# Two mixer entries of a fused transformer kernel: sums of squares by halves, a diagonal of roots, and vector lengths by products with ones

## What is computed

```python
x = x + hybrid_mixer(rmsnorm(x, norm_g[layer, 1]), ...)
def rmsnorm(x, g):
    y = xf * lax.rsqrt(jnp.mean(xf * xf, axis=-1, keepdims=True) + EPS)
    return y.astype(x.dtype) * g
```

```python
f = swiglu_ffn(rmsnorm_2(x, ffn1_norm_pre[i]), ffn1_w_in[i], ffn1_w_out[i])
x = x + 0.5 * rmsnorm_2(f, ffn1_norm_post[i])
h = rmsnorm_2(x, mix_norm_pre[i])
p = h @ mix_w_in[i]
...
def l2norm(x):
    return x * lax.rsqrt(jnp.sum(x * x, axis=-1, keepdims=True) + 1e-6)
q = l2norm(q.reshape(b, l, GDN_HEADS, GDN_DK)) * (GDN_DK ** -0.5)
k = l2norm(k.reshape(b, l, GDN_HEADS, GDN_DK))
```

## Time and profile before

| | |
|---|---|
| median of 3 runs | 2804.7 us (2804.18 to 2805.13) |
| the profiled execution | 2807.67 us |
| its span in the trace | 2805.9 us |
| TensorE busy | 2735.0 us, 97% |
| ScalarE / VectorE / GpSimd busy | 1459.5 / 1588.1 / 899.6 us |
| mean granted clock of TensorE | 0.99 |
| HBM read | 446.06 MB, 159 GB/s over the span |

### The profile page before, as it was taken

How to read it: one execution, slowest core, us unless ns; L and a number is a source line. 1 busy time by engine, 2 the same in 40 slices (tenths; PEclk the granted TensorE clock), 3 DMA queues, 4 the chain that set the end, 5 groups by cost and what they waited for, 6 DMA issues and landing times.

```text
span 2805.9 us, 46606 instructions
## 1 busy us (share of the span) xinstructions
PE 2735.0 (97%) x17368; PEld 2363.6 (84%) x17368; DVE 1588.1 (57%) x2439; ACT 1459.5 (52%) x2134; POOL 899.6 (32%) x469
## 2 busy tenths in 40 slices
PE   9999999999999999999989999999999899999999
PEld 7879897888878997878879898878788798998787
DVE  5543854545535845545546586555455465856554
ACT  5545655445444655445445644655454456446543
POOL 0017663000027665010037554710100375547200
PEclk9999999999999999999999999999999999999999
DMA  6655445655555446656557542466565575424664
GB/s 215 186 176 147 136 150 173 187 180 181 187 161 155 133 148 194 187 173 192 187 136 195 114 91 77 147 193 186 180 188 187 136 195 113 91 71 144 193 187 143
DMA packets 368442, 450.01 MB, mean 160 GB/s; under 512 B 32526, under 2 KB 266128, under 8 KB 368240
## 3 DMA queue, kind: packets, MB, share of 16 engines
q1 hardware_dynamic: 366768, 445.82, 54.4%
q10 hardware_dynamic: 544, 0.95, 0.1%
q0 software_dynamic: 928, 0.45, 0.1%
HBM read 446.06 MB, written 1.05 MB: 159 GB/s over the span
## 4 chain that ended last, share of the span: by engine, by line
PE 90%; DVE 4%; ACT 3%; POOL 2%; issue 1%; DMA 0%; SPq 0%; DVEq 0%; ACTq 0%
PE PS L515 27%; PE PS L517 26%; PE PS L516 26%; POOL wl L551 2%; PE PS L671 1%; DVE PS L2119 1%; ACT wh L543 1%; PE PS L1082 1%; PE PS L648 1%; PE PS L1149 1%; ACT xh L1290 1%; PE PS L780 1%; PE PS L1017 1%; PE PS L1008 1%; PE PS L1139 1%
## 5 line engine op out<-in xcount | busy, mean ns | idle before, releaser
L551 POOL TENSOR_TENSOR wl<-ring,wh 128x1024 fp32r<-128x1024 f32 (+1 forms) x348 | 835.6, 2419 | 1706.5 <-ACT wh L543 1705.2
L543 ACT ACTIVATE wh<-ring 128x1024 fp32r<-128x1024 f32 x848 | 890.8, 1056 | 906.5 <-PE PS L515 863.7
L551 DVE TENSOR_TENSOR wl<-ring,wh 128x1024 fp32r<-128x1024 f32 x500 | 611.4, 1225 | 620.4 <-ACT wh L543 620.1
L515 PE MATMUL PS<-wh,xh 128*128 128x512 f32 x1600 | 633.0, 396 | 22.3 <-DVE xl L1807 14.0
L517 PE MATMUL PS<-wh,xl 128*128 128x512 f32 x1600 | 622.5, 389 | 0.0
L516 PE MATMUL PS<-wl,xh 128*128 128x512 f32 x1600 | 621.6, 389 | 0.0
L515 PE MATMUL PS<-xh,wh 128*128 128x256 f32 x1888 | 554.9, 294 | 1.8 <-DVE xl L1807 1.7
L516 PE MATMUL PS<-xl,wh 128*128 128x256 f32 x1888 | 539.6, 286 | 0.0
L517 PE MATMUL PS<-xh,wl 128*128 128x256 f32 x1888 | 539.5, 286 | 0.0
L515 PEld LDWEIGHTS PS<-xh,wh 128*128 128x128 f32 x1888 | 367.4, 195 | 22.8 <-issue 16.1
L515 PEld LDWEIGHTS PS<-wh,xh 128*128 128x128 f32 x1600 | 301.0, 188 | 88.6 <-issue 20.6
(11 more groups left out here) (294 smaller groups left out, 2615.4 us busy)
## 6 DMA issues: line engine op xcount, KB each, us to landing
ring<-in_ffn_w_in_dram SPq DMA_DIRECT2D x352, 256.0 KB, 3.0
ring<-in_mix_w_in_dram SPq DMA_DIRECT2D x256, 256.0 KB, 3.8
ring<-in_w_in_dram SPq DMA_DIRECT2D x200, 256.0 KB, 3.0
ring<-in_ffn_w_gate_dram SPq DMA_DIRECT2D x176, 256.0 KB, 2.9
ring<-in_ffn_w_up_dram SPq DMA_DIRECT2D x176, 256.0 KB, 3.1
ring<-in_ffn_w_down_dram SPq DMA_DIRECT2D x176, 256.0 KB, 2.7
ring<-in_ffn_w_out_dram SPq DMA_DIRECT2D x176, 256.0 KB, 2.8
ring<-in_w_branch_dram SPq DMA_DIRECT2D x32, 256.0 KB, 2.8
```

The lines of the kernel that those rows point to most:

```text
L515: first_ = mm(o, w[0], x[0], start=start, stop=False, skip_group_check=True)
L543: act_(dst, src, ACT.Copy).then_inc(hi_ready, 1)
L551: (engine or v_).tensor_tensor(dst, src, part_views(t, wh)[0], ALU.subtract).then_inc(lo[t.slot()], 1)
```

## The change

- The sum of squares of a tile is taken in two halves of 512 columns, in the mixers' entries and in `act_post`. The first half's sum gets the constant eps by an Identity and is then the bias of the Ln over the second half's sum. In `dve_post` each half's product with `post` waits for its own half's square.
- `dve_scale` goes. ScalarE multiplies the identity by the roots (a diagonal, 128x128, in `sq`), and TensorE computes each block as a product of `x` with this diagonal in place of a transposition of the scaled tile.
- In the second mixer's entry one of the two `high` moves behind the second tile's `stats`.
- The lengths: a product of a 128x128 matrix of ones with two heads' squares gives the sums on all partitions at once, in bank 4, twice per group (after the first and after the second tile). ScalarE takes Ln and Exp over 128x512 in place, and `unit` reads the bank. `pick` and `spread` go. The table load stands ahead of the wait for the sums. VectorE's `short` is cut in two, with the first `unit` between.

```diff
+        def diag(q):
+            return sqt[:, q, 0:P]
...
-        def pe_xt_mix(pe, s, m):
-            for q in range(QT):
-                pe_xt(pe, s, q, sqt, lambda h: pe.wait_ge(xn_made, 4 * m + 2 * q + 1 + h))
+        def pe_xt_mix(pe, s, tr, q):
+            pe.wait_ge(tr[1].sem, tr[1].at(f"mix.{q}.diag"))
+            for k in range(KB):
+                ins = mm(xt_bank(q, k), x[:, q, k * P:(k + 1) * P], diag(q), start=True, stop=True)
+                if k % 4 == 3:
+                    ins.then_inc(xt_done, 1)
...
-            def sums(n):
+            def sums(j):
+                n = j // 2
                 pe.wait_ge(m2[1].sem, m2[1].at(f"l2sq{n}"))
...
-                for h in range(4):
-                    ins = mm(PS[0:4, 4, 0:S], pick[:, 3 - h:7 - h], sq[:, 4 * (n % 2) + h, :], start=(h == 0), stop=(h == 3))
-                ins.then_inc(m2[0].sem, m2[0].did(f"l2s{n}"))
-            def spread(j):
...
                     pe.wait_ge(m2[2].sem, m2[2].at(f"l2n{j - 1}"))
...
+                mm(bank(4), ones, sqp(2 * (n % 2) + j % 2), start=True, stop=True).then_inc(
+                    m2[0].sem, m2[0].did(f"l2s{j}"))
...
-                group(f"QKV{n}", (n + 1) % 2 * 2, {0: lambda: sums(n - 2), 2: lambda: spread(2 * n - 4), 3: lambda: spread(2 * n - 3)})
+                group(f"QKV{n}", (n + 1) % 2 * 2, {0: lambda: sums(2 * n - 4), 1: lambda: sums(2 * n - 3)})
...
-            act_sum(e, tr, f"{tag}.ss{q}", 2 + q, PS[:, 2 * q:2 * q + 2, :].rearrange("p b n -> p (b n)"),
-                    act2.rearrange("p a q c -> p (a q c)"), scale * D ** -0.5)
-            act_root(e, tr, lay, f"{tag}.ss{q}", f"{tag}.{q}", 2 + q, 1, consts[:, 2:3])
+                col = 2 + q if h else 6 + q
+                act_sum(e, tr, f"{tag}.ss{q}.{h}", col, bank(2 * q + h), means[:, h * HALF:(h + 1) * HALF], scale * D ** -0.5)
+                if h == 0:
+                    e.wait_ge(tr[1].sem, tr[1].at(f"{tag}.ss{q}.0", lay))
+                    act_(ss[:, col:col + 1], ss[:, col:col + 1], ACT.Identity, bias=consts[:, 0:1]).then_inc(
+                        tr[1].sem, tr[1].did(f"{tag}.se{q}"))
...
             def stats(q):
-                e.wait_ge(x_upd, 4 * s + 2 * q + 2)
-                act_sum(e, tr, f"mix.ss{q}", q, x[:, q, :], sqt[:, q, :], D ** -0.5)
-                act_root(e, tr, lay, f"mix.ss{q}", f"mix.{q}", q)
+                halves = ((4 + q, slice(0, HALF)), (q, slice(HALF, D)))
+                for h, (col, at) in enumerate(halves):
+                    e.wait_ge(x_upd, 4 * s + 2 * q + 1 + h)
+                    act_sum(e, tr, f"mix.ss{q}.{h}", col, x[:, q, at], sqt[:, q, at], D ** -0.5)
...
+                act_(r_, ss[:, q:q + 1], ACT.Ln, bias=ss[:, 4 + q:5 + q]).then_inc(tr[1].sem, tr[1].did(f"mix.{q}.ln"))
...
+                act_(r_, r_, ACT.Exp, scale=-0.5).then_inc(tr[1].sem, tr[1].did(f"mix.{q}.rstd"))
+                e.wait_ge(tr[1].sem, tr[1].at(f"mix.{q}.rstd"))
+                act_(diag(q), ident[:], ACT.Copy, scale=r_).then_inc(tr[1].sem, tr[1].did(f"mix.{q}.diag"))
             if post:
                 post(0)
-                high(e, t, 2)
+                high(e, t, 1)
                 stats(0)
                 post(1)
                 act_xh(e, s, 0, range(4), gain)
                 stats(1)
+                high(e, t, 1)
                 act_xh(e, s, 0, range(4, KB), gain)
...
-            def root(n):
-                e.wait_ge(m2[0].sem, m2[0].at(f"l2s{n}"))
...
-                tables(LN_EXP)
-                r_ = rstd[0:4, 0, 0:S]
-                act_(r_, PS[0:4, 4, 0:S], ACT.Ln, bias=consts[0:4, 0:1]).then_inc(m2[1].sem, m2[1].did(f"l2.{n}.ln"))
...
+            def root(j):
+                e.wait_ge(m2[0].sem, m2[0].at(f"l2s{j}"))
+                act_(bank(4), bank(4), ACT.Ln, bias=consts[:, 0:1]).then_inc(m2[1].sem, m2[1].did(f"l2.{j}.ln"))
...
             for n in range(6):
                 high(e, t, 1)
                 if n >= 2:
-                    root(n - 2)
-                high(e, t, 2)
+                    tables(LN_EXP)
+                    root(2 * n - 4)
+                high(e, t, 1)
+                if n >= 2:
+                    root(2 * n - 3)
+                high(e, t, 1)
+                if n >= 2:
+                    tables(SILU_TANH)
...
-        def dve_scale(e, tr, q):
...
-                short(n)
+                short(n, (0,))
                 if 1 <= n <= 4:
                     unit(2 * n - 2)
+                short(n, (2,))
+                if 1 <= n <= 4:
                     taps(2)
                     unit(2 * n - 1)
                     taps(3)
```

More of the change, by code:

```diff
@@ L199, in program @@
         post = sb("post", [D])
-        ss = sb("ss", [4])
+        ss = sb("ss", [8])
         rs = sb("rs", [4])
@@ L224, in program @@
         ones64, rot = masks[:, 6 * P:7 * P], masks[:, 7 * P:8 * P]
-        pick = sb("pick", [7])
         W = sb("W", [WIDE])
@@ L798, in pe_mix1 @@
                                 if (q, m) == (0, 1):
-                                    pe_xt(pe, s, 1, sqt, lambda h: pe.wait_ge(xn_made, 4 * lay + 2 + 1 + h))
+                                    pe_xt_mix(pe, s, first["norm"], 1)
                         t.k += 4
@@ L1247, in _ @@
                 pe_ffn(pe, t, first["ffn"], s, "f0", 1)
-                pe_xt(pe, s + 1, 0, sqt, lambda h: pe.wait_ge(xn_made, 4 * env.lay + 1 + h))
+                pe_xt_mix(pe, s + 1, first["norm"], 0)
                 pe_mix1(pe, t, first["mix"], first["soft"], s + 1, lay)
@@ L1258, in _ @@
                 pe_ffn(pe, t, second["ffn"], s, "f0", 2)
-                pe_xt_mix(pe, s + 1, LAYERS + lay)
+                for q in range(QT):
+                    pe_xt_mix(pe, s + 1, second["norm"], q)
                 pe_mix2(pe, t, s + 1)
@@ L1317, in act_mix_in @@
+            r_ = rs[:, 2 + q:3 + q]
+            e.wait_ge(tr[1].sem, tr[1].at(f"{tag}.ss{q}.1", lay))
+            act_(r_, ss[:, 2 + q:3 + q], ACT.Ln, bias=ss[:, 6 + q:7 + q]).then_inc(tr[1].sem, tr[1].did(f"{tag}.{q}.ln"))
+            e.wait_ge(tr[1].sem, tr[1].at(f"{tag}.{q}.ln", lay))
+            act_(r_, r_, ACT.Exp, scale=-0.5, bias=consts[:, 2:3]).then_inc(tr[1].sem, tr[1].did(f"{tag}.{q}.rstd"))
         def act_mix_in(e, t, tr, s, gain, post=None):
-            lay = env.lay
             def stats(q):
-                e.wait_ge(x_upd, 4 * s + 2 * q + 2)
-                act_sum(e, tr, f"mix.ss{q}", q, x[:, q, :], sqt[:, q, :], D ** -0.5)
-                act_root(e, tr, lay, f"mix.ss{q}", f"mix.{q}", q)
+                halves = ((4 + q, slice(0, HALF)), (q, slice(HALF, D)))
+                for h, (col, at) in enumerate(halves):
+                    e.wait_ge(x_upd, 4 * s + 2 * q + 1 + h)
+                    act_sum(e, tr, f"mix.ss{q}.{h}", col, x[:, q, at], sqt[:, q, at], D ** -0.5)
+                    if h == 0:
+                        e.wait_ge(tr[1].sem, tr[1].at(f"mix.ss{q}.0"))
+                        act_(ss[:, col:col + 1], ss[:, col:col + 1], ACT.Identity, bias=consts[:, 0:1]).then_inc(
+                            tr[1].sem, tr[1].did(f"mix.se{q}"))
+                r_ = rs[:, q:q + 1]
+                e.wait_ge(tr[1].sem, tr[1].at(f"mix.ss{q}.1"))
+                act_(r_, ss[:, q:q + 1], ACT.Ln, bias=ss[:, 4 + q:5 + q]).then_inc(tr[1].sem, tr[1].did(f"mix.{q}.ln"))
+                e.wait_ge(tr[1].sem, tr[1].at(f"mix.{q}.ln"))
+                act_(r_, r_, ACT.Exp, scale=-0.5).then_inc(tr[1].sem, tr[1].did(f"mix.{q}.rstd"))
+                e.wait_ge(tr[1].sem, tr[1].at(f"mix.{q}.rstd"))
+                act_(diag(q), ident[:], ACT.Copy, scale=r_).then_inc(tr[1].sem, tr[1].did(f"mix.{q}.diag"))
@@ L1518, in square @@
                 if n >= 2:
[L1519 removed]
+                    e.wait_ge(m2[0].sem, m2[0].at(f"l2s{2 * n - 3}"))
                 e.wait_ge(m2[1].sem, m2[1].at(f"silu{n}"))
@@ L1794, in step @@
             e.wait_ge(tr[2].sem, tr[2].at(name))
-        def dve_scale(e, tr, q):
-            e.wait_ge(tr[1].sem, tr[1].at(f"mix.{q}.rstd"))
-            for b in (2 * q, 2 * q + 1):
-                v_.tensor_scalar(tok(sqt, b), tok(x, b), rs[:, q:q + 1], None, ALU.mult).then_inc(xn_made, 1)
         def dve_xl(e, s, q, ks, gain):
@@ L2052, in dve_setup @@
             v_.memset(consts[:, 3:4], -0.5 * math.log(P))
-            v_.memset(pick, 0.0).then_inc(pro_dve.sem, pro_dve.did("pick0"))
-            e.wait_ge(pro_dve.sem, pro_dve.at("pick0"))
-            v_.memset(pick[:, 3:4], 1.0)
             v_.memset(consts[:, 1:2], LN_EPS).then_inc(pro_dve.sem, pro_dve.did("consts"))
@@ L2137, in gated, with short @@
                                                 ALU.mult), f"glu.{num}.{b}")
-            def short(n):
+            def short(n, b0s=(0, 2)):
                 e.wait_ge(m2[1].sem, m2[1].at(f"cp.QKV{n}"))
-                for b0 in (0, 2):
+                for b0 in b0s:
                     for tap in range(CTAPS):
@@ L2158, in unit @@
             def unit(j):
```

(2 more changed lines are left out.)

29 lines of the change are left out of this document (7 added, 22 removed).

## The result

The changed kernel takes 2780.97 us (median of 4 runs, 2778.03 to 2783.55) against 2804.86 us for the kernel before on the same chip (4 runs, 2804.18 to 2805.13): a ratio of 0.9915, with a 95% interval of 0.9898 to 0.9932. The forecast was 2781.2. The profiled execution of the changed kernel took 2779.34 us, its span is 2777.5.

A forecast was written before the change was run, and what follows sets the result against it. TensorE, busy for 97% of the span, was taken to bound the kernel. Terms -19.3 + 1.8 - 3.4 - 0.6 - 1.0 - 1.0 gave -23.5 us, from a median of 2804.7 to 2781.2 us, range 2774.5 to 2789.5.

The forecast's parts named there:

- Groups, -19.3: Eight projection groups of the second mixer: cheaper sums and spreads on TensorE save 2.41 us each, 19.3 us in all.
- 0.3 of switching: Projection group: some 0.3 us of switching counted within TensorE's 16.0 us per group, which was to become 13.6.
- ScalarE's loop, 13.2 against 13.6: Projection groups: ScalarE's work between second sums takes 13.2 us, shorter than TensorE's 13.6, so nothing is charged.
- The cover: Projection groups: the slack of ScalarE's sequence against TensorE's time per group, put at 0.4 us.
- The first rival: Projection groups: ScalarE's sequence binds, say at 15 us, so a group shrinks by only 1.0 us; 2792.5 us, chance 0.10.
- First mixer's entries, +1.8: First mixer's two entries: products start at the same time, but eight fp32 products cost 0.9 us more than transposes each entry.
- Second mixer's entries, -3.4: Second mixer's two entries: removed scalings, moved high part and halves shorten the chain by 1.7 us each.
- The rival of the clock: Second mixer's entries: the clock stays up, bringing up to 2 us more per entry; 2777.2 us, chance 0.15.
- its "against": Second mixer's entries: second tile's wait stays near 3 us and GpSimd's two low parts cap the full-clock gain.
- FFN entries and end, -0.6 and -1.0: Three FFN entries with `post` save 0.2 us each by halves; the program's end saves a product and half a square.
- Clock elsewhere, -1.0: Low-clock stretches, as behind the last group: removing the spread may spare one per layer; -1.0 us, from +3.4 to -3.4.
- The factor of two: Mixer entries: the trace prices an fp32 product at 0.22 us against 0.11 for a transpose; the skill's rule says four times.

The follow-up runs named there:

- spare_products: Changed kernel with four unread 512-column products between the two tiles' diagonal products at the second mixer's entries: 2777.9 us.
- all_second_transposed: Changed kernel with both tiles of the second mixer's entries again scaled on VectorE and transposed, halves and moved high part kept: 2777.09 us.
- high_ahead: Changed kernel with the moved high part back ahead of the first tile's statistics at the second mixer's entry: 2784.06 us.
- whole_squares: Changed kernel with each row's sum of squares again in one activation over 1024 columns, at all entries and for `post`: 2783.95 us.
- The combination: Changed kernel with scaling and transposes at all mixer entries; at the second mixer's, four spare products and one low part on VectorE: 2773.84 us.
- repeat: Changed kernel unaltered, run once more on the same chip as the run that combined several edits: 2780.55 us.
- first_transposed: Changed kernel with the first mixer's two entries again scaled on VectorE and transposed, halves of the squares kept: 2778.23 us.

## Why the prediction came out

The total held (2781.2 against 2780.97), partly because errors of its steps cancel.

- **Groups, -19.3.** The mechanism was right, the size small: -21.4. The product with ones costs 0.85 us and not 0.90 (the lower bound's row was the exact one), and what went was worth 2.67 + 1.70 = 4.37 us a group and not 4.21. The "0.3 of switching" that the forecast kept in its group did not stay: the period is 13.27, not 13.6.
- **ScalarE's loop, 13.2 against 13.6.** TensorE binds, as said, but barely. With 0.52 us more in ScalarE's loop the second products recur after 13.67 to 13.76 us, so the loop is 13.2 us: the forecast's own sum. The cover was about 0.03 and not 0.4, because the other side of the comparison, TensorE's 13.6, was too long. The first rival was nearer than its 0.10 suggests: nearly any longer loop would have made it real, though 0.2 us more would cost only that much at each of six places.
- **First mixer's entries, +1.8.** Measured +2.2, 1.09 an entry: the eight products with what follows cost 0.96 (0.90 forecast), and they start 0.13 us later (forecast: "the same time, within 0.1 us"). The size was nearly right, but not for the reason given. ScalarE's first square to the second tile's products took 3.02 us before (203.66 to 206.68), with a scaling held up behind GpSimd; it takes 2.69 in the change (204.12 to 206.81) and 2.18 with the whole square (203.37 to 205.55). So the two parts' prices hang on each other: the diagonal costs 0.58 us an entry beside whole squares and 1.17 beside halves, the halves 0.51 beside the diagonal and nothing beside transposes.
- **Second mixer's entries, -3.4.** Measured -1.8. The chain up to the tiles was right: the first tile's products start 2.56 us nearer the FFN's end (2.8 forecast), the second's 2.03 (2.6), and the first weight product 1.06, inside the forecast's 0.8 to 1.9. The term that was mis-sized is the eight products of the second tile, priced at 1.8 us, the price at full clock; the forecast itself placed this stretch at 1.2 GHz. They took up to 3.79. With the clock held up (`spare_products`) the entries are worth 1.8 and 1.5 us, about the forecast's 1.7, so what the sum lacked is the price of the low clock. Also wrong was the credit: the removed scalings were to bring the most, and bring nothing beside the moved high part (`all_second_transposed`).
- **The rival of the clock.** It came true in part: the low stretch shrank from 10.2 us to 6.8 and 3.4, and with spare work in the wait it is gone, worth 0.9 and 0.6 us an entry where the rival had up to 2. GpSimd's low parts and VectorE's cap the rest, as its "against" said. Products in place of transposes and a shorter low stretch mostly go together here: 10.2 us or more with transposes in both tiles, 6.8 with one tile transposed, 6.8 or less with the diagonal in both. The Trainium skill (TensorE: Matmul & The Clock Gate, Part 4) says that transposes don't count as busy in the same way, and these rows agree in direction. The exceptions are an entry of `high_ahead` and one of `whole_squares`, with the diagonal in both tiles and 10.2 us, where the tiles' products start later. The combination shows that transposes do no harm when other products stand beside them.
- **FFN entries and end, -0.6 and -1.0.** Measured -0.2 (the three waits sum to 0.72 us, 0.95 before) and -0.83. `whole_squares` shows the end's share to be the halves' alone.
- **Clock elsewhere, -1.0.** The terms read from the ledger give +2.2 - 1.8 - 21.4 - 0.2 - 0.8 = -22.0, the medians -23.9 and -24.7 (repeat), so -1.9 to -2.7 are left to it. The profiled executions differ by more, -28.4 and -25.0, through stretches of 3.4 us that come and go. The forecast's "Removing the spread may spare one per layer" was so in both profiles of the changed kernel: the stretch right behind the last group (1598.8 in the earlier trace rows, and 2370.2 in the second layer) is gone in both layers. The one that starts at 1598.4 in the changed kernel's trace stands 9 us behind the last group and answers to one at 1609.0 before (windows below). Over all profiles a stretch starts within 2 us of the last group's end in 6 of 24 places with the new lengths and in 3 of 4 with the old. The products with an operand of 8 rows stand there in all of them. Why low stretches are fewer with the new lengths stays open.
- **The factor of two** between a product with the diagonal and a transposition held at full clock: eight take 2.05 us against 1.09 by their rows. The Trainium skill (TensorE: Matmul & The Clock Gate, Terms) has four times; the estimate by it, +5.3 for the two first entries, did not come.

The windows of the changed kernel behind its last group; the granted clock stands third from the right:

```profile
1589.00:1598.00 9.00, 9.00 (x74) 8.64 (x73) 8.07 (x21) 3.30 (x6) 0.47 (x1) 1.00 0.21 64
1598.40:1601.80 3.40, 3.40 (x18) 3.40 (x17) 0.89 (x3) 3.40 (x7) 2.35 (x2) 0.50 0.00 0
```

## What to carry to other kernels

Read a change with several parts as a ledger of shifts between two traces: here one half gave all 24 us and the other nothing, and within the other a loss of about 3 us by the diagonal hid a gain of the same size by halves and order. A price found by taking one part out holds beside the parts that stay: the halves cost 0.5 us beside the diagonal and nothing beside the transposes. Work moved from another engine onto the one that binds is paid in full, and at half clock nearly twice (2.05 and 3.79 us for the same eight products); price it with the clock of the very stretch. Where that engine waits, and its clock falls, spare products in the wait can be worth more than a shorter chain.

## What the runs showed of the hardware

**VectorE's scaling waits for GpSimd.** The forecast took 2.47 us for two scalings, of which one takes 0.48 by the median, as they stood, with no cause. GpSimd's timeline of the kernel before at that place has it: two low parts run from 1442.88 to 1447.57, and the first scaling, started at 1445.78 and 2071 ns long, ends 0.3 us behind them.

```profile
1442.88 4.69 POOL L551 TENSOR_TENSOR wl<-ring,wh 128x1024 fp32r<-128x1024 f32 x2 [3.27 <-ACT wh L543]
```

In `all_second_transposed` the moved high part leaves one low part ahead, which ends at 1446.19, and the two scalings take 0.98 us (GpSimd's, then VectorE's timeline):

```profile
1443.82 2.37 POOL L550 TENSOR_TENSOR wl<-ring,wh 128x1024 fp32r<-128x1024 f32 x1 [3.22 <-ACT wh L542]
```

```profile
1445.89 0.98 DVE L1832 TENSOR_SCALAR sq<-x,rs 128x512 f32<-128x512 f32 x2 [1.85 <-ACT rs L1347]
```

The Trainium skill (SBUF — State Buffer, Who interferes with whom) has VectorE's two-port modes and GpSimd block each other for a whole instruction; these rows agree, and so do those of the first mixer (first scaling 1.24 us, ending 0.3 us behind a low part, against 0.48). So the moved high part had a second use: it cleared the scaling's way. That every scaling here runs in such a mode was not tested by itself.

**The clock** fell to half in each second mixer's entry of every profiled execution but those of `spare_products` and `combined`, and the second one of `first_transposed`. How late it falls and for how long varies between executions of one kernel: in the repeat of the changed kernel the second entry's low stretch lasted 6.8 us, where it had been 3.4.
